# Input projection over four prompt tiles and one tile that holds the samples' high and low halves side by side

## The chip, the cores and the metric

The kernel runs on one core of one Trainium2 chip. The metric is the device time of one execution in microseconds (us), as the median of several runs. The matrix engine is TensorE (PE in the profile, PEld its loads of the stationary operand), the others are VectorE (DVE), ScalarE (ACT), GpSimd (POOL) and SyncE (SP), which here only issues DMA transfers.

## The reference, cut to what matters

The reference is one step of a decoder layer for 512 prompt tokens and 64 sample tokens (8 sequences of 8). Both groups go through the same weights:

```python
def mix_inputs(x, pos, g_attn, w_in, w_gate_up, b_gate):
    xn = rms_norm(x, g_attn)
    gq, gk, gv, gr, ga, sq, sk, sv = split_cols(xn @ w_in)     # 2048 x 4368 weights
    ...
    log_a = log_sigmoid(ga @ w_gate_up + b_gate) / GLA_TAU
    sq, sk = rope(sq, pos), rope(sk, pos)

def layer_sample(...):
    q, k, v, log_a, gr, sq, sk, sv = mix_inputs(...)
    o_gla, s_fin = gla_recurrent(q, k, v, log_a, s_gla)        # linear attention with a state
    o_swa, new_k, new_v = swa_sample(sq, sk, sv, c_k, c_v, attn_sinks)   # window attention with a cache
    ...
```

Then come an output projection, a second norm, and a layer of 16384 experts of which 128 per token are chosen. All is in float32. The change touches the product `xn @ w_in` and the place where the sample attention reads its rows.

## The kernel before, in words

The kernel runs stage after stage: norm and transpose, input projection (`project`), attention of the prompt, attention of the samples (`attend`, called twice), output projection, expert queries, routing, experts, final norm. Each stage ends with a barrier of all engines.

**High and low halves.** TensorE multiplies in a rounded float32 format. To keep float32 accuracy each operand is split into a high part (the value rounded by a ScalarE copy) and a low part (the rest, by a subtraction). A product is three passes: high x high, high x low, low x high (`PASSES`); low x low is left out. `product` (L104) runs over 16 chunks of 128 of the contraction and issues 48 matmuls that all add into one bank of PSUM.

**The projection** (L237 and below). The 4368 output columns are cut into 14 slices of 312. The 576 tokens, kept transposed in `c.act[HI]` and `c.act[LO]`, are the stationary operand: five tiles of 128 tokens, at a stride of 112 (`STRIDE`), so that neighbouring tiles overlap by 16 tokens (4 x 112 + 128 = 576). The weights' slice moves, 312 columns at a time. Per slice PE does 5 tiles x 48 matmuls. SP loads the raw weights of the next slice; ACT makes the high half of them (L284), DVE the low half (L297). DVE copies each finished bank to `out` (L306), and GpSimd stores it into the scratch array `proj` in DRAM (L271): 112 rows of tiles 0 to 3, 128 of tile 4, so that no row is stored twice. PE waits for `split` (the slice's halves) at the start of a slice and for `moved` (the bank is free) before a tile; its waits come in program order.

**The sample attention** (`attend(nc, c, "sample")`). SP loads the samples' 64 rows of `proj` into `cur` in four pieces (L684): columns GA0..V0 (gate input, q, k), SQ0..SV0 (window queries and keys) together with a small table for the rotation, V0..SQ0 (v and output gate), SV0..PROJ (window values). Each piece has a semaphore (`qk_here`, `s_here`, `vr_here`, `sv_here`). ACT issues ten small loads of constants in the meantime. DVE clears two tiles (L900, L901) and then waits for all constants; PE waits for them as well, transposes the gate input (L1098), and DVE copies it (L914): from there a chain of gate logarithms, sums, exponentials (ACT), a reciprocal of 64 x 1024 (L931) and products (L936 to L939) runs on DVE, until PE computes with the recurrent state (L1139, L1147). GpSimd rotates the window queries and keys (L764, six steps). The recurrent state, 4 MB, is loaded to `state` by SP (L712) after the constants and `vr_here`.

Of the kernel before, what the change touches and what calls it, by code (L numbers as in the profile page):

```python
# [5 lines left out]
ALU = mybir.AluOpType  # L6
# [3 lines left out]
F32R = mybir.dt.float32r  # L10
U32 = mybir.dt.uint32

P = 128
D = 2048
KC = D // P
SEQ = 512
DEC_BATCH, DEC_SEQ = 8, 8
SAMPLES = DEC_BATCH * DEC_SEQ
TOKENS = SEQ + SAMPLES
PROMPT_TILES = SEQ // P  # L20
TILES = 5
STRIDE = (TOKENS - P) // (TILES - 1)
W_IN_SLICES = 14
HALF = TOKENS // 2
HI, LO = 0, 1
# [8 lines left out]
SWA_HEADS, HD, KV = 16, 64, 2  # L34
# [5 lines left out]
GA0 = 0  # L40
Q0 = GA0 + GATE_RANK
K0 = Q0 + GLA_HEADS * DK
V0 = K0 + GLA_HEADS * DK
R0 = V0 + GLA_HEADS * DV
SQ0 = R0 + GLA_HEADS * DV
SK0 = SQ0 + SWA_HEADS * HD
SV0 = SK0 + KV * HD
PROJ = SV0 + KV * HD
# [46 lines left out]
def in_pairs(eng, count, step):  # L95

    with eng.Fori(0, count // 2 - 1) as i:
        for s in range(2):
            step(i * 2 + s, s, True)
    for s in range(2):  # L100
        step(count - 2 + s, s, s == 0)


def product(pe, out, stationary, moving):  # L104

    for k in range(KC):
        for n, (a, b) in enumerate(PASSES):
            last = pe.matmul(out, stationary(a, k), moving(b, k), start=(k == 0 and n == 0),  # L108
                             stop=(k == KC - 1 and n == len(PASSES) - 1))
    return last  # L110
# [123 lines left out]
            each_tile(pe, turn)  # L234


def project(nc, c, name, weights, first, dst):  # L237

    ctx, sb, sem = stage(nc)
    with ctx:
        slices, cols = weights.shape[0], weights.shape[3]
        raw = [first[0], sb(name + "_raw", [P, KC, cols])]
        w = [[first[1 + part], sb(name + tag, [P, KC, cols], F32R)] for part, tag in ((HI, "_hi"), (LO, "_lo"))]
        out = sb(name + "_out", [P, TILES, cols])
        raw_here = [sem(f"{name}_raw_here{s}") for s in range(2)]
        rounded, split = sem(name + "_rounded"), sem(name + "_split")
        stored, out_free = [[sem(f"{name}_{x}{t}") for t in range(TILES)] for x in ("stored", "out_free")]  # L250
        summed, moved = sem(name + "_summed"), sem(name + "_moved")
        block = ctx.enter_context(nc.Block())

        @block.sync
        def _(sp):
            def load(n, s, more):
                if more:
                    sp.wait_ge(split, n + 1)
                    sp.sem_inc(c.held, 1)
                    sp.dma_start(raw[1 - s][:, :, :], weights[bass.ds(n + 1, 1)].rearrange("a p k n -> (a p) k n")).then_inc(raw_here[1 - s], 16)  # L260

            in_pairs(sp, slices, load)

        @block.gpsimd
        def _(pool):
            def store(n, s, more):
                for t in range(TILES):
                    rows = P if t == TILES - 1 else STRIDE
                    pool.wait_ge(moved, n * TILES + (TILES + t + 1))
                    pool.sem_inc(c.held, 1)  # L270
                    pool.dma_start(dst[t * STRIDE:t * STRIDE + rows, bass.ds(n * cols, cols)], out[0:rows, t, :]).then_inc(stored[t], 16)  # L271
                for t in range(TILES):
                    pool.wait_ge(stored[t], n * 16 + 16)
                    pool.sem_inc(out_free[t], 1)

            in_pairs(pool, slices, store)

        @block.scalar
        def _(act):
            def hi(n, s, more):  # L280
                if more:
                    act.wait_ge(raw_here[1 - s], n * 8 + (16 - 8 * s))
                    act.wait_ge(summed, n * TILES + 2 * TILES)
                    act.activation(w[HI][1 - s][:, :, :], raw[1 - s][:, :, :], ACT.Copy).then_inc(rounded, 1)  # L284

            in_pairs(act, slices, hi)

        @block.vector
        def _(dve):
            dve.sem_inc(split, 2)  # L290
            dve.sem_inc(moved, TILES)
            for t in range(TILES):
                dve.sem_inc(out_free[t], 1)

            def lo(n, s):
                dve.wait_ge(rounded, n)
                dve.tensor_tensor(w[LO][s][:, :, :], raw[s][:, :, :], w[HI][s][:, :, :].bitcast(F32),  # L297
                                  ALU.subtract).then_inc(split, 1)

            def move(n, s, more):  # L300
                if more:
                    lo(n + 1, 1 - s)
                for t in range(TILES):
                    dve.wait_ge(out_free[t], n + 1)
                    dve.wait_ge(summed, n * TILES + (2 * TILES + t + 1))
                    dve.tensor_copy(out[:, t, :], c.bank[:, t, 0:cols]).then_inc(moved, 1)  # L306

            in_pairs(dve, slices, move)

        @block.tensor  # L310
        def _(pe):
            pe.sem_inc(summed, 2 * TILES)

            def products(n, s, more):
                pe.wait_ge(split, n + 2)
                for t in range(TILES):
                    pe.wait_ge(moved, n * TILES + (t + 1))
                    product(pe, c.bank[:, t, 0:cols], lambda part, k: c.act[part][:, k, t * STRIDE:t * STRIDE + P],
                            lambda part, k: w[part][s][:, k, :]).then_inc(summed, 1)

            in_pairs(pe, slices, products)

# [154 lines left out]
def attend(nc, c, kind):  # L477
# [15 lines left out]
    def sb(name, shape, dt=F32):  # L493
        return sb_(kind + "_" + name, shape, dt)

    def sem(name, n=1):

        s = sem_(kind + "_" + name)
        per[id(s)] = n
        return s  # L500

    with ctx:
# [46 lines left out]
        else:  # L549
# [6 lines left out]
            k2 = sb("k2", [P, 2, KV, 2, HD])  # L556
            k2_old = sb("k2_old", [DEC_SEQ, 2, KV, 2, HD])

        const_here = sem("const_here")


# [31 lines left out]

        block = ctx.enter_context(nc.Block())
        b0, b2, b3, b7 = (c.bank[:, n, :] for n in (0, 2, 3, 7))

        def wait(eng, s, i, n=None):

# [80 lines left out]
        def _(sp):  # L679
            def load(t, dst, src, here, first, end):  # L680

                at = bass.ds(t * P, P) if prompt else slice(SEQ, TOKENS)
                sp.sem_inc(c.held, 1)
                sp.dma_start(dst[0:T, first:end], src[at, first:end]).then_inc(here, 16)  # L684

            def load_swa(t):
                load(t, cur, c.d.proj, s_here, SQ0, SV0)
                load(t, trig, c.d.trig, s_here, 0, HD)

            load(0, cur, c.d.proj, qk_here, GA0, V0)  # L690
            load_swa(0)
            load(0, cur, c.d.proj, vr_here, V0, SQ0)
            load(0, cur, c.d.proj, sv_here, SV0, PROJ)
            if prompt:
                with sp.Fori(0, turns - 1) as i:
                    wait(sp, rope_step, i)
                    load_swa(i + 1)
                    wait(sp, gated, i)
                    wait(sp, er_ready, i)
                    load(i + 1, cur, c.d.proj, qk_here, GA0, V0)  # L700
                    wait(sp, o_ready, i)
                    wait(sp, silu_ready, i)
                    load(i + 1, cur, c.d.proj, vr_here, V0, SQ0)
                    wait(sp, kept, i)
                    load(i + 1, cur, c.d.proj, sv_here, SV0, PROJ)
                for s in (gla_heads_ready, swa_heads_ready, kept, state_ready):
                    wait(sp, s, turns - 1)
            else:
                sp.wait_ge(const_here, all_consts)
                sp.wait_ge(vr_here, 16)  # L710
                sp.sem_inc(c.held, 1)
                sp.dma_start(state[:], c.d.state_in.rearrange("b h d v -> d b h v")).then_inc(old_here, 16)  # L712
                for dst, src in ((k_old, ck), (v_old, cv)):
                    sp.dma_start(dst[:], src[:, 0:DEC_SEQ, :].rearrange("b t f -> t b f")).then_inc(old_here, 16)
                for dst, src in ((k_new, ck), (v_new, cv)):
                    sp.dma_start(dst[0:WINDOW - DEC_SEQ, :, :],
                                 src[:, DEC_SEQ:WINDOW, :].rearrange("b t f -> t b f")).then_inc(old_here, 16)
# [24 lines left out]
        def _(pool):  # L742
# [45 lines left out]
            def turn(i, more):  # L788
# [13 lines left out]
                pool.tensor_copy(mask[:, :], mask_all[:, :]).then_inc(kept, 1)  # L802
                end_turn(pool, i)

            rope(0)
            if prompt:
                with pool.Fori(0, turns - 1) as i:
# [91 lines left out]
        def _(dve):  # L899
            dve.memset(ga_t[:, :], 1.0).then_inc(first_ready, 1)  # L900
            dve.memset(q_spread[:, :, :], 0.0).then_inc(first_ready, 1)  # L901
            if prompt:
                dve.memset(state[:, 0, :, :], 0.0).then_inc(first_ready, 1)
                dve.memset(k_t[:, :, 0:WINDOW], 0.0).then_inc(first_ready, 1)
            dve.wait_ge(const_here, all_consts)
            dve.wait_ge(first_ready, 5 if prompt else 2)
            dve.sem_inc(c.held, 1)
# [1424 lines left out]
```

## Time and profile before

| what | value |
|---|---|
| median of 3 runs | 4011.97 us (4008.87 to 4014.4) |
| the profiled execution | 4016.56 us, its span 4014.9 us |
| PE busy | 3706.2 us, 92% of the span |
| DVE, ACT, POOL busy | 61%, 30%, 48% |
| projection's matmuls | from 53.8 to 537.4 us |
| prompt attention | from about 547 to 800 us |
| sample attention | from about 800 us to about 940 us |

A stage of this kernel begins when the last engine of the stage before has ended, so its time is that of the chain that ends last in it. In the profile "L108" is the line of the matmul in the helper `product`, "128*128" after it the rows and columns of the stationary operand, and "128x312" the moving one. "PEclk" is the clock granted to TensorE as a share of full speed (1.00 is 2.4 GHz, 0.50 is 1.2 GHz).

### The profile page before, as it was taken

The numbers are of one execution on the slowest core, as the hardware profiler recorded it, in microseconds if no ns is written. First come the engines' busy times: TensorE is split into PE (matmuls) and PEld (weight loads), VectorE is DVE, ScalarE is ACT, GpSimd is POOL, SyncE is SP. The second block draws the span as 40 slices with busy tenths as digits, with TensorE's granted clock in tenths as the row PEclk, the third lists the DMA queues.
The fourth block names the chain that finished last, engine by engine and source line by source line (L and its number), as shares of the span: only waits on it lengthen the run. The fifth ranks groups of instructions, "written<-read, shape, count | busy, mean of one in ns | idle before, by whom it ended". The sixth has DMA issues, their size and how long they took to land. (4 is left out here: it accounts for less than half of the span.)

```text
span 4014.9 us, 68430 instructions
## 1 busy us (share of the span) xinstructions
PE 3706.2 (92%) x26360; PEld 3625.3 (90%) x26360; DVE 2429.9 (61%) x3100; ACT 1222.9 (30%) x1291; POOL 1944.7 (48%) x1188
## 2 busy tenths in 40 slices
PE   6999966668969999999999999999999999999995
PEld 6999955547969999999999999999999999999995
DVE  5222235540031999444445887888887887888886
ACT  3111123311221445444443333333323333333322
POOL 1000032213432999988883545544554555555551
PEclk8999977768989999999999999999999999999998
DMA  4222111042312656555557888888888888888877
GB/s 163 98 98 96 47 50 42 22 119 106 131 67 80 210 193 212 194 215 205 198 204 262 304 314 308 313 305 304 320 305 295 315 325 308 313 307 303 321 283 246
DMA packets 255947, 853.25 MB, mean 213 GB/s; under 512 B 26816, under 2 KB 109440, under 8 KB 182626
## 3 DMA queue, kind: packets, MB, share of 16 engines
q1 hardware_dynamic: 183662, 544.96, 38.6%
q0 software_dynamic: 48704, 282.27, 18.1%
q10 hardware_dynamic: 23476, 24.61, 1.8%
q8 instruction: 67, 1.10, 0.1%
q14 instruction: 38, 0.31, 0.0%
HBM read 787.50 MB, written 64.20 MB: 212 GB/s over the span
## 5 line engine op out<-in xcount | busy, mean ns | idle before, releaser
L1882 POOL DMA_INDIRECT fetched<-in_v,at x256 | 526.9, 2058 | 636.7 <-DVE total L1999 583.1
L1999 DVE SCALAR_TENSOR_TENSOR total<-fetched,coef_s,total 128x2048 f32<-128x2048 f32 x256 | 600.8, 2347 | 76.8 <-issue 66.4
L2067 PE MATMUL bank<-coef_hi,act_hi 128*128 128x320 f32 x2048 | 633.9, 310 | 11.2 <-DVE y_t L2005 5.6
L2067 PE MATMUL bank<-coef_hi,act_lo 128*128 128x320 f32 x2048 | 632.5, 309 | 0.0
L2067 PE MATMUL bank<-coef_lo,act_hi 128*128 128x320 f32 x2048 | 632.4, 309 | 0.0
L1886 POOL DMA_INDIRECT hot_s<-hot_scratch,at x256 | 399.6, 1561 | 241.3 <-DVE coef_s L1992 164.2
L2067 PEld LDWEIGHTS bank<-coef_hi,act_hi 128*128 128x128 f32 x2048 | 384.7, 188 | 12.7 <-DVE act_lo L1975 6.1
L1934 ACT ACTIVATE hot<-bank 128x320 f32<-128x320 f32 x128 | 55.9, 437 | 1112.7 <-PE bank L108 1103.6
L1559 POOL TENSOR_SCALAR rt_first<-rt_number,picks_t 128x128 f32<-128x128 f32 x320 | 356.1, 1128 | 66.9 <-PE bank L1765 66.8
L108 PE MATMUL bank<-act_hi,first_hi 128*128 128x320 f32 (+1 forms) x1152 | 354.6, 308 | 34.7 <-DVEq L1332 30.3
L2067 PEld LDWEIGHTS bank<-coef_lo,act_hi 128*128 128x128 f32 x2048 | 384.6, 188 | 0.0
L2067 PEld LDWEIGHTS bank<-coef_hi,act_lo 128*128 128x128 f32 x2048 | 384.5, 188 | 0.0
L1975 DVE TENSOR_TENSOR act_lo<-raw_v,act_hi 128x2048 fp32r<-128x2048 f32 x128 | 293.5, 2293 | 132.5 <-ACT act_hi L1930 132.4
L108 PE MATMUL bank<-act_lo,first_hi 128*128 128x320 f32 (+1 forms) x1152 | 354.4, 308 | 0.0
L108 PE MATMUL bank<-act_hi,first_lo 128*128 128x320 f32 (+1 forms) x1152 | 354.0, 307 | 0.0
L108 PE MATMUL bank<-act_lo,other_hi 128*128 128x320 f32 (+1 forms) x1152 | 352.9, 306 | 0.0
L108 PE MATMUL bank<-act_hi,other_hi 128*128 128x320 f32 (+1 forms) x1152 | 352.8, 306 | 0.0
L108 PE MATMUL bank<-act_hi,other_lo 128*128 128x320 f32 (+1 forms) x1152 | 352.7, 306 | 0.0
L1750 PE MATMUL bank<-act_hi,first_hi 128*128 128x256 f32 x1024 | 289.8, 283 | 7.0 <-POOL first_lo L1550 3.9
L1750 PE MATMUL bank<-act_hi,other_hi 128*128 128x256 f32 x1024 | 287.3, 281 | 0.1
L1750 PE MATMUL bank<-act_hi,first_lo 128*128 128x256 f32 x1024 | 287.0, 280 | 0.0
L1750 PE MATMUL bank<-act_lo,first_hi 128*128 128x256 f32 x1024 | 286.9, 280 | 0.0
(390 smaller groups left out, 9694.8 us busy)
## 6 DMA issues: line engine op xcount, KB each, us to landing
raw_v<-in_v SPq DMA_DIRECT2D x128, 1024.0 KB, 6.7
first_raw<-in_u_t SPq DMA_DIRECT2D x107, 1024.0 KB, 5.0
other_raw<-in_u_t SPq DMA_DIRECT2D x106, 1024.0 KB, 5.2
rt_raw<-in_u_t SPq DMA_DIRECT2D x43, 1024.0 KB, 5.0
gates_scratch<-rt_space SPq DMA_DIRECT2D x5, 4096.0 KB, 12.2
gates<-gates_scratch SPq DMA_DIRECT2D x64, 320.0 KB, 7.2
proj_raw<-in_w_in SPq DMA_DIRECT2D x7, 2496.0 KB, 10.0
mh_raw<-in_w_out SPq DMA_DIRECT2D x16, 1024.0 KB, 4.8
```

Source lines behind the costliest of these rows:

```text
L108: last = pe.matmul(out, stationary(a, k), moving(b, k), start=(k == 0 and n == 0), stop=(k == KC - 1 and n == len(PASSES) - 1))
L1559: last = pool.tensor_scalar(first[:, n % 2, t, :], number[:, :], c.picks_t[:, 0, at:at + 1], c.picks_t[:, 2, at:at + 1], ALU.is_equal, ALU ...
L1750: last = pe.matmul(c.bank[:, 5 + s, 0:SPARSE], u[a][s][:, k, :], c.act[b][:, k, 0:SPARSE], start=(k == 0 and n == 0), stop=(k == KC - 1 an ...
L1882: pool.indirect_dma_start(fetched[:, k % 2, :], None, c.d.v, bass.IndirectOffsetOnAxis(ap=at[:, s, k:k + 1], axis=0)).then_inc(fetched_her ...
L1886: pool.indirect_dma_start(hot_s[:, k:k + 1], None, row_elements, bass.IndirectOffsetOnAxis(ap=at[:, s, FETCH + k:FETCH + k + 1], axis=0)). ...
L1934: act.activation(hot[:, r, :], c.bank[:, r % 2, 0:DENSE], ACT.Gelu).then_inc(hot_ready, 1)
L1975: dve.tensor_tensor(v_slot(LO, s), raw_v[:, s].rearrange("e r (a d) -> e (r a) d", d=SPARSE), v_slot(HI, s).bitcast(F32), ALU.subtract).th ...
L1999: dve.scalar_tensor_tensor(out=total[:, :], in0=fetched[:, k % 2, :], scalar=coef_s[:, k:k + 1], in1=total[:, :], op0=ALU.mult, op1=ALU.ad ...
L2067: last = pe.matmul(c.bank[:, 4 + m, 0:DENSE], v_chunk(a, q % 2, r, m), coef[z][:, r, :], start=(r == 0 and n == 0), stop=(r == ROWS - 1 an ...
```

## The change

- The tiles of the projection no longer overlap: tiles 0 to 3 are prompt tokens 0..511, in tiles of 128, with `product` as before.
- Tile 4 is for the 64 samples alone. Two GpSimd copies build `pair`, for each of the 16 chunks the samples' high half in columns 0..63 and their low half in columns 64..127. One matmul of `pair` against the weights' high half gives high x high in PSUM rows 0..63 and low x high in rows 64..127. A second matmul, of the 64 high columns against the weights' low half, adds high x low to rows 0..63. So there are 32 matmuls instead of 48 for this tile.
- The lower rows (low x high) aren't added there. They are stored in a second piece of scratch (`sample_low`, over the array `gates`), by one more DMA per slice.
- The sample attention loads both parts, the second into `low_part` (over the tile of the recurrent state), and adds them in four pieces: two on DVE, two on GpSimd. `qk_here`, `vr_here`, `s_here` and `sv_here` are now signalled by these additions, and the load of the state waits for all four.

```diff
+def sample_low(c):
+    return c.d.gates[0].rearrange("j i t -> (j i t)")[0:SAMPLES * PROJ].rearrange("(t n) -> t n", n=PROJ)
...
         @block.gpsimd
         def _(pool):
             def store(n, s, more):
                 for t in range(TILES):
-                    rows = P if t == TILES - 1 else STRIDE
+                    rows = SAMPLES if t == PROMPT_TILES else P
...
+                    if t == PROMPT_TILES:
+                        pool.dma_start(sample_low(c)[:, bass.ds(n * cols, cols)], out[SAMPLES:P, t, :]).then_inc(stored[t], 16)
...
+            for part in (HI, LO):
+                pool.tensor_copy(pair[:, :, part * SAMPLES:(part + 1) * SAMPLES], c.act[part][:, :, SEQ:TOKENS]).then_inc(paired, 1)
             in_pairs(pool, slices, store)
...
         @block.tensor
         def _(pe):
+            pe.wait_ge(paired, 2)
             pe.sem_inc(summed, 2 * TILES)
+
+            def sample_product(s):
+                both, upper = c.bank[:, PROMPT_TILES, 0:cols], c.bank[0:SAMPLES, PROMPT_TILES, 0:cols]
+                for k in range(KC):
+                    first, last = k == 0, k == KC - 1
+                    if last:
+                        pe.matmul(upper, c.act[HI][:, k, SEQ:TOKENS], w[LO][s][:, k, :], start=False, stop=False)
+                    done = pe.matmul(both, pair[:, k, :], w[HI][s][:, k, :], start=first, stop=last)
+                    if not last:
+                        pe.matmul(upper, c.act[HI][:, k, SEQ:TOKENS], w[LO][s][:, k, :], start=False, stop=False)
+                return done
...
-                    product(pe, c.bank[:, t, 0:cols], lambda part, k: c.act[part][:, k, t * STRIDE:t * STRIDE + P],
-                            lambda part, k: w[part][s][:, k, :]).then_inc(summed, 1)
+                    if t < PROMPT_TILES:
+                        last = product(pe, c.bank[:, t, 0:cols], lambda part, k: c.act[part][:, k, t * P:(t + 1) * P],
+                                       lambda part, k: w[part][s][:, k, :])
+                    else:
+                        last = sample_product(s)
+                    last.then_inc(summed, 1)
...
+        def add_parts(eng, first, end, here):
+            eng.wait_ge(parts_here[first], 32)
+            eng.tensor_tensor(cur[0:T, first:end], cur[0:T, first:end], low_part[:, first:end], ALU.add).then_inc(here, 16)
...
+            def load_parts(first, end):
+                sp.dma_start(cur[0:T, first:end], c.d.proj[SEQ:TOKENS, first:end]).then_inc(parts_here[first], 16)
+                sp.dma_start(low_part[:, first:end], sample_low(c)[:, first:end]).then_inc(parts_here[first], 16)
...
+            else:
+                load_parts(GA0, V0)
+                load_parts(SQ0, SV0)
+                load(0, trig, c.d.trig, s_here, 0, HD)
+                load_parts(V0, SQ0)
+                load_parts(SV0, PROJ)
...
                 sp.wait_ge(const_here, all_consts)
+                sp.wait_ge(qk_here, 16)
+                sp.wait_ge(s_here, 32)
                 sp.wait_ge(vr_here, 16)
+                sp.wait_ge(sv_here, 16)
...
+            if not prompt:
+                add_parts(pool, SQ0, SV0, s_here)
+                add_parts(pool, SV0, PROJ, sv_here)
             rope(0)
...
+            else:
+                add_parts(dve, GA0, V0, qk_here)
+                add_parts(dve, V0, SQ0, vr_here)
             dve.wait_ge(const_here, all_consts)
```

## Rows read from the trace of the kernel before

**Rows 1.** Stretches: us, busy (count) of PE PEld DVE ACT POOL; PEclk, DMA share, GB/s.
```profile
53.80:58.80 5.00, 4.98 (x19) 4.99 (x20) 0.00 (x0) 0.00 (x0) 0.00 (x0) 0.50 0.83 304
58.80:537.40 478.60, 478.57 (x3343) 478.31 (x3341) 101.72 (x82) 56.96 (x13) 37.39 (x69) 1.00 0.24 87
```

**Rows 2.** Timeline of PE around 839: start, us, engine, line, shapes.
```profile
838.70 0.59 PE L1139 MATMUL bank<-sample_state,sample_q_spread 128*64 128x256 f32 x2
...
838.91 0.38 PE L1139 MATMUL bank<-sample_state,sample_q_spread 128*64 128x256 f32 x1
839.22 0.43 PE L1137 MATMUL bank<-sample_cur,sample_inner 64*64 64x256 f32 x1
...
839.49 0.38 PE L1137 MATMUL bank<-sample_cur,sample_inner 64*64 64x256 f32 x1
```

**Rows 3.** Timeline of PE around 852, same columns.
```profile
851.73 0.48 PE L1147 MATMUL bank<-sample_cur,sample_spare 64*128 64x256 f32 x1
...
852.05 0.38 PE L1147 MATMUL bank<-sample_cur,sample_spare 64*128 64x256 f32 x1
```

**Rows 4.** Timeline of PE and its weight loads around 670 and 822.
```profile
669.84 0.27 PE L1159 MATMUL bank<-ident,prompt_o_norm 128*128 128x128 f32 x1
670.04 0.34 PE L1247 MATMUL bank<-prompt_probs_t,prompt_v_before 128*64 128x128 f32 x2
...
821.10 1.06 PE L1107 MATMUL bank<-sample_log_a,sample_suf 64*64 64x512 f32 x1
...
821.95 1.06 PE L1107 MATMUL bank<-sample_log_a,sample_suf 64*64 64x512 f32 x1
822.94 0.38 PE L1109 MATMUL bank<-sample_ind,sample_log_a 64*128 64x8 f32 x1
...
822.94 0.28 PEld L1109 LDWEIGHTS bank<-sample_ind,sample_log_a 64*128 64x128 f32 x1 [1.61 <-issue]
```

**Rows 5.** Timeline of PE around 902, transposes.
```profile
902.19 0.42 PE L1231 MATMUL bank<-ident,sample_scores 128*128 128x128 f32 x1
902.40 0.42 PE L1233 MATMUL bank<-ident,sample_scores 128*8 128x128 f32 x1
```

**Rows 6.** Timeline of PE around 906, pairs of short matmuls.
```profile
906.36 0.30 PE L1258 MATMUL bank<-sample_spare,sample_v_old 8*64 8x32 f32 x2
906.59 0.24 PE L1256 MATMUL bank<-sample_spare,sample_v_new 128*64 128x32 f32 x1
```

**Rows 7.** GpSimd's copies (groups by form: count, busy us, mean ns), its last store.
```profile
L801 POOL COPY prompt_k_t<-prompt_k_t 128x256 f32<-128x256 f32 x4 | 1.6, 403 | 0.0
...
L800 POOL COPY prompt_v_before<-prompt_cur 128x128 f32<-128x128 f32 x4 | 1.2, 291 | 56.0 <-PE bank L1248 56.0
...
538.56 0.56 POOL L271 DMA_DIRECT2D proj_scratch<-proj_out  x1 [6.36 <-DVE proj_out L306]
```

**Rows 8.** Sample attention: a load, landings, DVE, stretches (as rows 9); a long subtraction.
```profile
802.98 1.19 SPq L684 DMA_DIRECT2D sample_cur<-proj_scratch  x2
...
DMA to landing us min/median/max: 4.0/6.2/6.2
...
811.35 0.21 DVE L914 COPY sample_ga_t<-bank 16x64 f32<-16x64 f32 x1 [8.00 <-PE bank L1098]
...
801.40:809.90 8.50, 0.00 (x0) 0.50 0.80 167
812.00:825.00 13.00, 7.05 (x14) 0.50 1.07 334
...
L1975 DVE TENSOR_TENSOR act_lo<-raw_v,act_hi 128x2048 fp32r<-128x2048 f32 x128 | 293.5, 2293 | 132.5 <-ACT act_hi L1930 132.4
```

**Rows 9.** Three stretches: us, PE busy (matmuls), PEclk, DMA share, GB/s.
```profile
838.60:852.30 13.70, 13.70 (x61) 1.00 0.24 70
857.50:860.95 3.45, 2.81 (x14) 1.00 0.00 0
860.95:864.40 3.45, 3.45 (x10) 0.50 0.00 0
```

More of the change, by code:

```diff
@@ L251, in project @@
         summed, moved = sem(name + "_summed"), sem(name + "_moved")
+        pair = sb(name + "_pair", [P, KC, 2 * SAMPLES], F32R)
+        paired = sem(name + "_paired")
         block = ctx.enter_context(nc.Block())
@@ L267, in store @@
                 for t in range(TILES):
-                    rows = P if t == TILES - 1 else STRIDE
+                    rows = SAMPLES if t == PROMPT_TILES else P
                     pool.wait_ge(moved, n * TILES + (TILES + t + 1))
                     pool.sem_inc(c.held, 1)
-                    pool.dma_start(dst[t * STRIDE:t * STRIDE + rows, bass.ds(n * cols, cols)], out[0:rows, t, :]).then_inc(stored[t], 16)
+                    pool.dma_start(dst[t * P:t * P + rows, bass.ds(n * cols, cols)], out[0:rows, t, :]).then_inc(stored[t], 16)
+                    if t == PROMPT_TILES:
+                        pool.dma_start(sample_low(c)[:, bass.ds(n * cols, cols)], out[SAMPLES:P, t, :]).then_inc(stored[t], 16)
                 for t in range(TILES):
-                    pool.wait_ge(stored[t], n * 16 + 16)
+                    pool.wait_ge(stored[t], n * 32 + 32 if t == PROMPT_TILES else n * 16 + 16)
                     pool.sem_inc(out_free[t], 1)
+            for part in (HI, LO):
+                pool.tensor_copy(pair[:, :, part * SAMPLES:(part + 1) * SAMPLES], c.act[part][:, :, SEQ:TOKENS]).then_inc(paired, 1)
             in_pairs(pool, slices, store)
@@ L557, in attend @@
             k2_old = sb("k2_old", [DEC_SEQ, 2, KV, 2, HD])
+            low_part = state[:, :, :, :].rearrange("p n h v -> p (n h v)")[0:T, 0:PROJ]
+            parts_here = {first: sem(f"part_here{first}") for first in (GA0, V0, SQ0, SV0)}
         const_here = sem("const_here")
@@ L688, in load_swa @@
                 load(t, trig, c.d.trig, s_here, 0, HD)
[L690 to L693, printed above, removed]
+            def load_parts(first, end):
+                sp.dma_start(cur[0:T, first:end], c.d.proj[SEQ:TOKENS, first:end]).then_inc(parts_here[first], 16)
+                sp.dma_start(low_part[:, first:end], sample_low(c)[:, first:end]).then_inc(parts_here[first], 16)
+            if prompt:
+                load(0, cur, c.d.proj, qk_here, GA0, V0)
+                load_swa(0)
+                load(0, cur, c.d.proj, vr_here, V0, SQ0)
+                load(0, cur, c.d.proj, sv_here, SV0, PROJ)
+            else:
[4 more added lines that the diff above has]
+                load_parts(SV0, PROJ)
             if prompt:
```

## The prediction

> **What bounds the kernel now.** I read the stretches of the input projection first, since that is where the change takes work away. Two stretches cover it [rows 1]: in the second the matrix engine (PE) is busy for 478.57 of 478.60 us, at a granted clock of 1.00, in 3343 matmuls, so one is issued every 478.6 / 3343 = 0.1432 us. Nothing else is near: in the same stretch VectorE is busy 101.72 us and GpSimd 37.39 us. PE's number of matmuls is this stage's time. Then I read PE's own timeline where the shape of the stationary operand changes from one matmul to the next [rows 2 to 4], because the new sample tile does that all the time and the old projection never does: all its matmuls are 128*128 (rows*columns of the stationary operand). Last I read the start of the sample attention, where the parts are added.
>
> **The projection: what goes.** Before, 14 slices x 5 tiles x 48 matmuls = 3360. After, a slice has 4 x 48 for the prompt and 32 for the samples (16 with the high and low halves side by side, 16 with the high half alone against the weights' low half). So 14 x 16 = 224 go: 224 x 0.1432 = **-32.1 us**, if the remaining ones keep the spacing.
>
> **The projection: what comes in.** In the sample tile, stationary operands of 128 columns and of 64 columns take turns. The order is both, upper, both, upper, and at the last k upper, both: 15 changes from 128 to 64 columns and 15 from 64 to 128 per slice. What does a change cost?
> - At full clock, matmuls of 64 columns follow each other every 0.21 to 0.22 us (838.70, 838.91; I reckon with 0.216). Then the rows of the operand change from 128 to 64, and the next starts 0.31 us later (839.22) and the one behind it 0.27 us after that (839.49) [rows 2]. A change thus costs about 0.093 before the first matmul of the new shape and 0.051 behind it, 0.144 us. I read it as: the next weights are not loaded while the last matmul still runs, but only after it. The row of the load says so too: at 822.94 a load starts together with its matmul after 1.61 us in which none was loaded [rows 4].
> - Into a 128-column operand the second part is larger: 851.73 to 852.05 is 0.32 us, 0.104 above 0.216 [rows 3]. So 0.093 + 0.104 = 0.197 us.
> - These change rows, or rows and columns. Two places change columns alone. At full clock 128*128 to 128*64 takes 0.20 us (669.84 to 670.04) behind transposes that at this clock should be spaced at about half their 0.213 us of the lower one [rows 4, 5]: +0.09 again. At the lower clock 64*64 to 64*128 takes 0.99 us (821.95 to 822.94) where the same work without a change takes 0.85 (821.10 to 821.95): +0.135 [rows 4]. So I take the change of columns at the price of the others.
>
> Per slice 15 x 0.144 + 15 x 0.197 = 5.12 us; x 14 = **+71.6 us**. The bounds: nothing per change [rows 5] (the first rival below), and 0.23 us, the time that two matmuls of 32 columns take together where each pair changes shape (906.36 to 906.59) [rows 6]; x 420 = 97 us. I take 71.6, as it comes from the rows nearest in moving length. Of the stage, -32.1 + 71.6 = +39.5 us, and a sample tile takes 32 x 0.143 + 5.12 = 9.7 us instead of 6.9.
>
> The Trainium skill has this rule (TensorEngine Tiling (Array Packing), Key Properties): a change of the tiling mode, as opposed to the tile alone, drains the engine. By that rule the trace agrees for every change of shape shown in rows 2 to 4. It gives no price. The same page (Restrictions) says that column tiling can't be had together with the transpose mode on 4-byte inputs, which would explain why rows 5, both transposes, show no such cost; no run here separates that yet.
>
> **The start of the projection.** PE now waits for two GpSimd copies of 128 x 1024 elements. It had started at 53.8 [rows 1]. COPY takes 0.291 us for 128 elements and 0.403 for 256 [rows 7]: 0.87 ns an element above a fixed part, so 1.07 us each and **+2.2 us** in all with the signal. Bounds: 1.2 (the lost time is at the lower clock [rows 1], 0.26 us a matmul against 0.143) and 3.3 (8 x 0.403). Queued behind the copies on GpSimd is only the first store, some 8 us later; behind PE's wait are the summed signal, thus ACT's conversion of the next slice, which waits for its load until 10 us later anyway. SP's load of the next slice isn't behind it.
>
> **Stores.** One more store per slice. A store's issue takes GpSimd 0.56 us [rows 7]; 13 of them lie under PE's work on the next slice, and DVE waits for out_free only a slice later. The last lies behind the last matmul: **+0.55 us** (0 to 1).
>
> **The prompt attention** reads the same rows of the same scratch: 0.
>
> **The sample attention.** Before, SP issues four loads of the projection (1.12 MB); those with V and R and the last are issued from 802.98 and land up to 6.2 us later, 809.2, at 167 GB/s in that stretch [rows 8]. DVE copies the gate inputs that PE turns at 811.35, just after the last constant is there [rows 8]. Now the low parts double the bytes: 1.09 MB more up to V and R. At 167 GB/s that is 6.5 us, at the 334 GB/s of the state load 3.3 us [rows 8]. So V and R land at 812.5 to 815.7. DVE adds them (64 x 2048 elements; 2.29 us by the row of the same length [rows 8]) before it waits for the constants, and only then copies its gates: 814.8 to 818.0, i.e. 3.5 to 6.6 us later. I take **+5.0 us**. The bounds: 0.2, if the transfers went no slower (809.2 + 2.3), and 10, if the add also waits for GpSimd, which now adds and rotates in the same time. Everything behind it shifts with it: the reciprocal and then qg, kg, ke are one chain on DVE. Two other waits move and stay under it. The state load is issued after the adds, not at 811; PE's first use of it is at the end of that same chain, so both shift by as much. GpSimd adds SQ..SV0 and the last 128 columns ahead of the rotation, whose keys SP needs only behind its cache loads, which come later too.
>
> **Sum.** -32.1 + 71.6 + 2.2 + 0.55 + 5.0 = +47.3 us. The profiled execution took 4016.56 us (4014.9 of it the span, 1.7 around it), so 4063.8 of its kind; the median of the runs shown is 4.6 lower, 4011.97, and with it **4059 us**.
>
> **Rivals.**
> - *The change of columns is free* (the price fails altogether). For it: alternating 128*128 and 128*8 operands run at 0.213 us each, without any gap [rows 5], and weights are loaded ahead there. Against: these are transposes, and rows 4 show the cost for columns in matmuls. Then -32.1 + 7.8 = -24.3: 3988 us, faster. It decides at 24.3 / 420 = 0.058 us per change: below that the kernel is faster.
> - *Half a price*: the engine waits for the end of the last matmul, but the weights' load hides in it. 420 x 0.093 = 39.1; -32.1 + 39.1 + 7.8 = +14.8: 4027 us. For it: no row shows a stream where each single matmul changes columns. Against: in rows 2 and 3 both parts are there.
> - *The clock falls in the sample tile.* With 9.7 us for 32 matmuls PE streams under half of the time there. For it: behind a stretch with 14 matmuls of half-filled rows in 3.45 us the granted clock fell from 1.00 to 0.50 [rows 9]. Against: in the stretch before, shapes changed too and it held at 1.00 over 13.7 us [rows 9]. The price: in 5.0 us at the lower clock 19 matmuls are done, 0.26 us each [rows 1], so 2.3 us are lost in each 5; one such fall per slice, up to two: 14 x 2.3 to 4.6 = 32 to 64 us more: 4091 to 4123, say 4107 us. The Trainium skill (TensorE: Matmul & The Clock Gate, Part 1) says that the clock is gated by how busy PE has been recently; rows 9 agree with that in kind.
>
> **Chances.** My forecast 0.50, clock falls 0.20, half a price 0.15, free 0.15. The forecast's own range, with the bounds of its terms, is 4035 to 4080. The range for 8 in 10 leaves out the free case and the top of the clock case: 4018 to 4120. A difference of 0.2% (8 us) is about what can be told from none. Faster by more: the free case, 0.15. Within: the lowest part of half a price, 0.04. Slower: 0.81.
>
> **What would show it.** In the changed kernel: 448 matmuls of the sample tiles, 224 of them with 64 columns; the next start 0.34 us behind a "both" (0.143 + 0.104 + 0.093) and 0.29 us behind an "upper" (0.143 + 0.051 + 0.093), or 0.143 behind each if the free rival is right; PE's weight loads starting with their matmul and not ahead of it; a sample tile of about 9.7 us; the stage ending at some 580 (537.4 + 2.2 + 39.5) instead of 513 with free changes; the granted clock at 1.00 through each slice, or 0.50 in each sample tile. At the sample attention, DVE's copy of the gates 5 us later against the stage's first load. I am wrong if the 128 to 64 change leaves the spacing as it is, or if ACT or DVE turn up as what PE waits for between slices.

## The result, and the profile of the changed kernel

The changed kernel takes **3998.26 us** (median of 6 runs, 3994.82 to 4004.03), the kernel before beside it 4013.02 (6 runs, 4008.87 to 4019.1): a ratio of 0.9962, interval 0.9952 to 0.9973. It is faster, by 10.8 to 19.3 us. The forecast was 4059 in a range of 4018 to 4120: wrong in sign, and outside the range.

PE alone between two weight shapes in a sample tile (after, the timeline of PE and of its weight loads; start, us, engine, line, shapes):

```profile
86.98 0.31 PE L333 MATMUL bank<-slice_hi,proj_pair 128*128 128x312 f32 x1
87.12 0.30 PE L335 MATMUL bank<-slice_lo,act_hi 128*64 128x312 f32 x1
87.27 0.31 PE L333 MATMUL bank<-slice_hi,proj_pair 128*128 128x312 f32 x1
...
86.98 0.13 PEld L335 LDWEIGHTS bank<-slice_lo,act_hi 128*64 128x64 f32 x1
87.13 0.19 PEld L333 LDWEIGHTS bank<-slice_hi,proj_pair 128*128 128x128 f32 x1
87.27 0.14 PEld L335 LDWEIGHTS bank<-slice_lo,act_hi 128*64 128x64 f32 x1
```

The matmuls start 0.14 to 0.15 us apart, at 128 columns and at 64, which is the spacing of the old projection [rows 1]. The weights of the next matmul are loaded when the one before it starts (the load for the matmul of 87.12 starts at 86.98), so PE never waits for them. Over the whole stage, the matmuls behind the 420 changes start 0.1429 us after the one before (mean of the trace at full clock). A change of columns costs nothing here, where the forecast had put 0.144 and 0.197 us.

The same in stretches (after; us, busy and count of each engine, granted clock, DMA share, GB/s). The first answers to the two of [rows 1] together, then the part at the lower clock and the rest:

```profile
56.10:508.70 452.60, 452.58 (x3136) 450.54 (x3136) 101.68 (x82) 56.90 (x13) 44.63 (x82) 0.99 0.26 97
...
56.11:61.50 5.39, 5.39 (x21) 5.39 (x22) 0.00 (x0) 0.00 (x0) 0.00 (x0) 0.50 0.98 419
61.50:508.70 447.20, 447.19 (x3117) 445.14 (x3116) 101.68 (x82) 56.90 (x13) 44.63 (x82) 1.00 0.26 93
...
86.00:90.70 4.70, 4.70 (x35) 4.57 (x34) 0.48 (x1) 0.00 (x0) 0.54 (x1) 1.00 0.10 34
```

There are 3136 matmuls instead of 3360, PE never pauses, 447.20 / 3117 = 0.1435 us each, and the clock holds at 1.00 through the sample tiles, so the rival with a falling clock did not happen either. From PE's first projection matmul to its last, the stage went from 483.55 us (53.82 to 537.37) to 452.58 (56.11 to 508.69), -31.0.

Where the rest of it went, read from the first and last matmul of each stage in the two timelines. The profiled span fell by 18.8 us (4014.9 to 3996.1):

| Term | forecast, us | measured, us |
|---|---|---|
| PE's start of the projection (53.82, 56.11) | +2.2 | +2.3 |
| 224 matmuls fewer | -32.1 | -31.0 |
| 420 changes of columns | +71.6 | in the line above |
| last projection matmul to the prompt attention's first (21.49, 23.38) | +0.55 | +1.9 |
| prompt attention (233.93, 233.16) | 0 | -0.8 |
| prompt's last matmul to the samples' last (134.44, 143.12) | +5.0 | +8.7 |
| sample attention's end to the head merge (15.29, 15.95) | 0 | +0.7 |
| sum at the head merge (942.52, 924.30) | +47.3 | -18.2 |

Only the third line decides the sign. Of the 31.0, 1.1 less than the 32.1 forecast, the shortfall lies in the prompt tiles: in the two traces their matmuls are 0.1432 us apart before and 0.1436 after, which is 1.1 us over 2680 of them. The kernels below that keep the sample tile's 32 matmuls as they are have 0.1436 too, the others 0.1431 to 0.1433; why is open. The line of the prompt attention can't be told from none: its code is unchanged, and in the traces of this document it takes between 233.2 and 236.1 us.

PE's start and the stores of the last slice (before, then after; timeline of GpSimd and PE):

```profile
53.82 0.62 PE L108 MATMUL bank<-slice_hi,act_hi 128*128 128x312 f32 x1 [7.43 <-DVEq L291]
...
53.60 1.04 POOL L286 CAST proj_pair<-act_hi 128x1024 fp32r<-128x1024 f32 x1 [6.17 <-POOLq L73]
54.59 1.03 POOL L286 CAST proj_pair<-act_lo 128x1024 fp32r<-128x1024 f32 x1
...
56.11 0.62 PE L108 MATMUL bank<-slice_hi,act_hi 128*128 128x312 f32 x1 [9.43 <-POOL proj_pair L286]
...
509.87 0.55 POOL L278 DMA_DIRECT2D proj_scratch<-proj_out  x1 [4.03 <-DVE proj_out L317]
510.41 0.55 POOL L280 DMA_DIRECT2D gates_scratch<-proj_out  x1
```

After, the second copy is what PE waited for last. 1.04 and 1.03 us are the 1.07 of the forecast. The bracket is PE's idle time since the last matmul of the norm stage, 7.43 us before and 9.43 after: the wait for the pair is worth 2.0 of the 2.3 us. The other 0.3 is in the norm stage, whose last matmul ends at 46.39 in the one profile and at 46.68 in the other.

The sample attention (before, timeline of SP's queue and DVE, then after, with GpSimd's last step of the rotation; these answer to [rows 8]):

```profile
800.82 1.42 SPq L684 DMA_DIRECT2D sample_cur<-proj_scratch  x2
...
818.60 0.68 DVE L924 TENSOR_TENSOR sample_log_a<-sample_low,sample_mag 64x512 f32<-64x512 f32 x1 [3.58 <-ACT sample_mag L828]
819.21 0.68 DVE L929 TENSOR_SCALAR sample_er<-sample_er 64x1024 f32<-64x1024 f32 x1
```
```profile
773.20 0.58 SPq L728 DMA_DIRECT2D sample_cur<-proj_scratch  x1
...
788.98 2.28 DVE L631 TENSOR_TENSOR sample_cur<-sample_cur,sample_state 64x2048 f32<-64x2048 f32 x1 [9.21 <-DMA sample_state<-gates_scratch]
791.19 0.20 DVE L971 COPY sample_ga_t<-bank 16x64 f32<-16x64 f32 x1
793.45 0.68 DVE L973 TENSOR_SCALAR sample_low<-bank 64x512 f32<-64x512 f32 x1 [2.06 <-PE bank L1158]
798.43 1.28 DVE L981 TENSOR_TENSOR sample_log_a<-sample_low,sample_mag 64x512 f32<-64x512 f32 x1 [3.58 <-ACT sample_mag L882]
799.65 1.88 DVE L986 TENSOR_SCALAR sample_er<-sample_er 64x1024 f32<-64x1024 f32 x1
...
799.35 1.63 POOL L815 TENSOR_TENSOR sample_roped<-sample_rt 64x576 f32<-64x576 f32 x1 [0.18 <-POOL sample_rt L815]
```

From the stage's first load to DVE's copy of the gates it is 17.99 us, before 10.53 (800.82 to 811.35): the addition of V and R waits 9.21 us for the low parts, takes 2.28 and only then lets the gates through. Behind that DVE's two operations at 798.43 and 799.65 took 1.28 and 1.88 us, where before both took 0.68.

### The profile page after: what moved, and what is told of

Its sections match the earlier page's. It is cut to its first block and busy times, and to the rows that moved or that the text cites. A ratio compares the mean times of both kernels' runs of the same rounds, so it can differ in the third digit from the quotient of the medians.

```text
span 3996.1 us, 68032 instructions
## 1 busy us (share of the span) xinstructions
PE 3679.9 (92%) x26136; PEld 3597.9 (90%) x26136; DVE 2435.8 (61%) x3102; ACT 1222.5 (31%) x1291; POOL 1938.9 (49%) x1206
## 5 line engine op out<-in xcount | busy, mean ns | idle before, releaser
L1943 POOL DMA_INDIRECT hot_s<-hot_scratch,at x256 | 381.2, 1489 | 241.2 <-DVE coef_s L2049 164.3
```

Of the source, the lines that this page charges most:

```text
L1943: pool.indirect_dma_start(hot_s[:, k:k + 1], None, row_elements, bass.IndirectOffsetOnAxis(ap=at[:, s, FETCH + k:FETCH + k + 1], axis=0)). ...
```

## The experiments

The forecast had read its price from matmuls that all work on full float32 operands, where the projection's are rounded to fp32r. In these profiles a full float32 matmul stands as two records, a rounded one as one. Two theories were to be told apart: *A*, the price belongs to full float32; *B*, it belongs to a change of the operand's rows, not of its columns. The two runs of shapes and the last one ran once each.

**Shapes with rounded operands.** The sample tile's 32 matmuls get other shapes, by turns (in even slices 128*128 with 64*128, then 64*128 with 64*64; in odd ones 128*64 with 64*64, then 128*128 with 64*64), with one full one at the end of the even slices and at the start of the odd ones; it leaves out part of the projection's sums.

```diff
-                    done = pe.matmul(both, pair[:, k, :], w[HI][s][:, k, :], start=first, stop=last)
...
+                for n, (rows, width) in enumerate(order):
+                    k = n // 2 % KC
+                    a, b = pair[0:rows, k, 0:width], w[HI][s][0:rows, k, :]
...
+                    done = pe.matmul(c.bank[0:width, PROMPT_TILES, 0:cols], a, b, start=n == 0, stop=n == len(order) - 1)
```

> The changed kernel, but the sample tile's 32 or 33 matmuls take other shapes, all on the rounded operands, so that the samples' projection is not computed. Even slices: 128*128 and 64*128 in turn (8 pairs), then 64*128 and 64*64 in turn (8 pairs). Odd slices: 128*64 and 64*64 in turn, then 128*128 and 64*64 in turn. Theory A (a change of shape costs only with operands in full float32, which is all that the trace of before showed it for; rounded operands pay nothing): 0.143 us from each start to the next in all four patterns, a tile of 4.6 to 4.8 us. Theory B (a change of the number of rows costs, in either format, a change of columns alone does not): 0.29 to 0.34 us at each change of rows, 0.143 in the pattern 64*128 / 64*64; the even tile some 7 us, the odd one 9 us, and the projection some 14 x 3.4 = 47 us longer than in the changed kernel.

4107.15 us. Its weight loads (timeline; the bracket is the idle time before a load):

```profile
88.57 0.19 PEld L335 LDWEIGHTS bank<-slice_hi,proj_pair 128*128 128x128 f32 x1 [0.15 <-issue]
88.91 0.18 PEld L335 LDWEIGHTS bank<-slice_hi,proj_pair 64*128 64x128 f32 x1 [0.15 <-issue]
89.25 0.19 PEld L335 LDWEIGHTS bank<-slice_hi,proj_pair 128*128 128x128 f32 x1 [0.15 <-issue]
...
286.40 0.13 PEld L335 LDWEIGHTS bank<-proj_hi,proj_pair 128*64 128x64 f32 x1 [0.16 <-issue]
286.69 0.13 PEld L335 LDWEIGHTS bank<-proj_hi,proj_pair 64*64 64x64 f32 x1 [0.15 <-issue]
```

Medians of start to start at full clock, over all slices: 338 and 337 ns between 128*128 and 64*128, 285 and 282 between 128*64 and 64*64, 337 and 283 between 128*128 and 64*64; but 141 and 146 between 64*128 and 64*64 (only 6 and 4 pairs, as most of that pattern ran at the lower clock) and 141 from 128*128 to 128*64 (7 pairs). A change of rows costs 0.14 to 0.20 us with rounded operands too, a change of columns alone nothing. *A* falls as the only reason; the price of the forecast, 0.144 and 0.197, is met for rows to within a few ns. The clock also fell, in the sample tile of every slice. The projection took 559.7 us instead of 452.6, where *B* had asked for some 47 more; the rest goes with the lower clock. The first fall (stretches):

```profile
82.00:92.00 10.00, 10.00 (x51) 7.67 (x50) 0.48 (x1) 0.00 (x0) 0.54 (x1) 1.00 0.14 51
92.00:99.00 7.00, 7.00 (x29) 6.33 (x27) 0.48 (x1) 2.42 (x1) 1.09 (x2) 0.51 0.03 6
```

**Shapes with full float32 operands.** The same edit with `a, b = a.bitcast(F32), b.bitcast(F32)`, and lists of shapes with changes of columns among them; it leaves out part of the sums too.

> The same with the operands read as full float32, where each matmul stands in the profile as two records (312 columns: 0.26 us each, by 0.216 for 256). Even slices: 128*128 and 128*64 in turn (8 pairs), then 64*128 and 64*64 in turn. Odd slices: eight 128*128, then 128*128 and 64*128 in turn (6 pairs), then 128*64 and 64*64 in turn (5 pairs). The samples' projection is not computed. Theory A: at each change, rows or columns, the starts lie 0.09 further apart before and 0.05 (into 64 columns) or 0.10 (into 128 columns) behind, 0.14 to 0.20 us per change, also for 128*128 / 128*64; none in the uniform eight. Theory B: no extra time in 128*128 / 128*64 nor in 64*128 / 64*64, only where the rows change.

4256.13 us. Without a change the records follow at 263 ns each. Weight loads where columns alone change:

```profile
299.58 0.19 PEld L335 LDWEIGHTS bank<-slice_hi,proj_pair 128*64 128x64 f32 x2 [0.42 <-issue]
300.25 0.30 PEld L335 LDWEIGHTS bank<-slice_hi,proj_pair 128*128 128x128 f32 x2 [0.48 <-issue]
```

One matmul of each shape takes 0.67 to 0.72 us instead of 0.53. In medians, the matmul of the new shape starts 356 ns behind the last one (+93) for 128*128 to 128*64 and for 128*64 to 128*128, 353 for 64*128 to 64*64, and 352 to 356 where rows change; its second record follows after 313 ns in a 128*64 operand (+50) and 367 in a 128*128 one (+104). So in full float32 columns cost as much as rows, in the very parts that the forecast took from [rows 2, 3]: 0.093, 0.051 and 0.104. *B* falls there. Together the two runs say: rows cost in both formats, columns only in full float32, and [rows 2 to 4], all full float32, could not show the difference. What it is about the format stays open: the transposes of [rows 5] also work on full float32, but are one record each, and they pay nothing for a change of columns (0.213 us at the lower clock, with or without a change).

The clock did not follow the changes of rows here. In all seven odd slices, where rows change by turns, it held at 1.00 through 20.7 us of sample tile. It fell in three of the even ones, and each time in the second half, where all operands have 64 rows.

The Trainium skill has one rule for both (TensorEngine Tiling (Array Packing), Key Properties): a change of the tiling mode drains the engine. Whether each shape of operand is a mode of its own, it doesn't say. Read so, as the forecast did, rows agree with it in both formats, columns in full float32; for columns with rounded operands the measurement says otherwise, and it decides.

**48 matmuls of 64 columns.** Back to before (and the edit is against before), except that the prompt tiles no longer overlap and the sample tile has 64 columns instead of 128: no halves side by side, no second store, the sample attention as before.

```diff
+            def sample_product(s):
...
+                return product(pe, c.bank[0:SAMPLES, PROMPT_TILES, 0:cols], lambda part, k: c.act[part][:, k, SEQ:TOKENS],
+                               lambda part, k: w[part][s][:, k, :])
```

> One part of the change alone: tiles of 128 prompt tokens and a sample tile of 64 columns, but with all three passes (48 matmuls, 128*64), no pair, no second scratch; the sample attention as in the kernel before. If a matmul of 64 stationary columns takes as long as one of 128 (0.143 us), nothing is gained without the side by side: 4013 us, within 0.1% of before, the projection 483.5 us. If fewer columns made it shorter (0.130 us = 312 columns at full clock), 672 x 0.013 = 9 us less, 4004 us.

4014.91 us against 4014.34 (10 and 15 runs), ratio 1.000, 0.9991 to 1.0009. The timeline of PE in a sample tile:

```profile
88.03 0.30 PE L108 MATMUL bank<-slice_hi,act_lo 128*64 128x312 f32 x1
88.17 0.30 PE L108 MATMUL bank<-slice_hi,act_hi 128*64 128x312 f32 x1
88.31 0.30 PE L108 MATMUL bank<-slice_lo,act_hi 128*64 128x312 f32 x1
```

A matmul takes the same with half its columns empty (0.142 against 0.143 us). The whole gain is in the number of matmuls, none in leaving out the overlap.

**Later wait for the pair.** PE's wait for the two copies moves from the stage's start to the first sample tile, four tiles later.

```diff
-            pe.wait_ge(paired, 2)
             pe.sem_inc(summed, 2 * TILES)
...
                     else:
+                        pe.wait_ge(paired, 2)
                         last = sample_product(s)
```

> The changed kernel, PE's wait for the pair moved from the start of the projection to just before the first sample tile, where the copies have long ended. If the wait is what lets PE start at 56.1 instead of 53.8, it starts at 53.8 again and all behind is 2.3 us earlier by the profile (1.2 if only the work at the lower clock is won): about 3996.5 us, ratio to before 0.9955 to 0.996. If the copies only took the place of another late arrival, nothing changes: 3998.5 us.

3996.90 us (3994.64 to 3998.59, 4 runs), ratio 0.9954, 0.9937 to 0.997. PE's first matmul (timeline):

```profile
54.70 0.62 PE L108 MATMUL bank<-slice_hi,act_hi 128*128 128x312 f32 x1 [7.42 <-DVEq L302]
```

PE's idle time ahead of it is 7.42 us, as before (7.43), against 9.43: by the profile the move gives back the whole 2.0 us of the wait. That the start isn't back at 53.82 lies ahead of it: in this profile the norm stage's last matmul ended at 47.28, in before's at 46.39. By the times it is 1.4 us, less than the intervals can tell.

**Transfers without additions, additions without transfers.** The 7.5 us at the sample attention are two costs in a row, transfers and an addition. One kernel loads all low parts and adds 16 elements of each; the other loads 16 elements of each (so every load is still issued) and makes the whole additions (with the high part added to itself). Their outputs miss the low parts.

```diff
-            eng.tensor_tensor(cur[0:T, first:end], cur[0:T, first:end], low_part[:, first:end], ALU.add).then_inc(here, 16)
+            eng.tensor_tensor(cur[0:T, first:first + 16], cur[0:T, first:first + 16], low_part[:, first:first + 16], ALU.add).then_inc(here, 16)
```
```diff
-                sp.dma_start(low_part[:, first:end], sample_low(c)[:, first:end]).then_inc(parts_here[first], 16)
+                sp.dma_start(low_part[:, first:first + 16], sample_low(c)[:, first:first + 16]).then_inc(parts_here[first], 16)
```

> The changed kernel, the low parts loaded as before, but each addition in the sample attention covers only the first 16 columns, so most of the low x high part is left out. Theory 'the transfers': DVE's copy of the gate inputs comes about 15.5 us behind the stage's first load instead of 17.9 (only the 2.3 us addition goes), and 10.5 in the kernel before; so the doubled loads are worth 5 of the 7.4 us. Theory 'the additions': it comes back to 11 us.

> The changed kernel, the additions at full width, but with the first part itself as second operand, and of the low parts only 16 columns each are loaded; the low x high part is left out. Theory 'the transfers': DVE's copy of the gate inputs comes about 12 to 13 us behind the stage's first load (10.5 and up to 2.3 for the addition). Theory 'the additions': 17 us. In both DVE's steps up to qg keep the 1.7 us by which GpSimd's shifted rotation lengthens them if that clash needs only the additions ahead of the rotation, and lose them if the rotation starts early enough again.

3996.15 and 3996.58 us, one run each. From each trace the first load of the stage and the copy of the gates, transfers alone first:

```profile
776.56 0.58 SPq L728 DMA_DIRECT2D sample_cur<-proj_scratch  x1
...
792.47 0.21 DVE L971 COPY sample_ga_t<-bank 16x64 f32<-16x64 f32 x1 [0.35 <-PE bank L1155]
```
```profile
775.21 0.58 SPq L728 DMA_DIRECT2D sample_cur<-proj_scratch  x1
...
788.13 0.20 DVE L971 COPY sample_ga_t<-bank 16x64 f32<-16x64 f32 x1
```

15.91 and 12.92 us, where before has 10.53 and after 17.99. Of the +7.5 the transfers are 5.4 and what is left, 2.1, is the addition; the additions alone give 2.4. The path from the gates' copy to the operation behind the reciprocal, 15.16 us before, is 16.84 in after and 16.73 and 16.78 in these two, but 15.16 in the joined kernel below. So this +1.7 comes with the later GpSimd rotation, which meets DVE's two operations (row at 799.35 above), and it stays when either part is made small.

**The low rows added in the projection (joined).** This takes away what the table of the changed kernel shows as losses. The sample tile comes second in the slice (ORDER = 0, 4, 1, 2, 3), its low rows are moved down by a transfer on the chip and added by GpSimd under PE's next tiles, one store goes out, and the sample attention is as before. PE waits for the pair only ahead of its first sample tile. The edit is against before.

```diff
+                    if t == PROMPT_TILES:
+                        pool.sem_inc(c.held, 1)
+                        pool.dma_start(low[:, :], out[SAMPLES:P, t, :]).then_inc(lowered, 16)
+                        pool.wait_ge(lowered, n * 16 + 16)
+                        pool.tensor_tensor(out[0:SAMPLES, t, :], out[0:SAMPLES, t, :], low[:, :], ALU.add).then_inc(joined, 1)
+                        pool.wait_ge(joined, n + 1)
```

> The 32 matmuls kept, the rest of the cost taken away: the sample tile is second in each slice, GpSimd moves its lower rows to rows 0..63 by a transfer within the chip, adds them there and stores one result, all behind PE's other tiles; PE waits for the pair only before that tile; the sample attention is that of the kernel before. If the changed kernel's gain of 31 us in the projection was eaten by 2.3 us of pair, about 1.9 at the end of the stage and 8.7 in the sample attention, this one gives 4013 - 31 = 3982 us (ratio 0.992), some 16 us below the changed kernel. If the sample attention's loss came from something else that also moved (clock phases, the placement of the barrier), it stays: 3990 us or more.

**3983.11 us** (3980.68 to 3987.16, 5 runs), ratio 0.9921, 0.9908 to 0.9935: by its interval 26 to 37 us below before, and below the changed kernel too. GpSimd and DVE (timeline), and the stretch of the projection with its part at the lower clock:

```profile
77.03 0.54 POOL L276 DMA_DIRECT2D table<-proj_out  x1
85.70 0.84 POOL L278 TENSOR_TENSOR proj_out<-proj_out,table 64x312 f32<-64x312 f32 x1 [8.14 <-DMA table<-proj_out]
...
783.74 0.21 DVE L943 COPY sample_ga_t<-bank 16x64 f32<-16x64 f32 x1 [8.39 <-PE bank L1127]
...
55.23:58.10 2.87, 2.87 (x11) 2.87 (x12) 0.00 (x0) 0.00 (x0) 1.51 (x2) 0.50 0.74 230
...
55.00:507.00 452.00, 451.50 (x3136) 449.53 (x3136) 101.78 (x83) 56.91 (x13) 58.88 (x99) 1.00 0.26 98
```

GpSimd waits 8.14 us for the transfer that it issued at 77.03. PE doesn't wait for it: the stage takes 451.50 us, the changed kernel's 452.58. The gates are copied 10.93 us behind the first load (before 10.53).

**More shapes with rounded operands.** Which changes are free, and is a matmul with few rows slow by itself? Even slices: 128*128 with 128*32 by turns, then 128*64 alone; odd slices: 64*128 alone, then 64*128 with 32*128. Part of the sums is left out again.

```diff
+                for n, (row, rows, at, width) in enumerate(order):
+                    k = n // 2 % KC
+                    a, b = pair[row:row + rows, k, at:at + width], w[HI][s][row:row + rows, k, :]
```

> The changed kernel with other shapes in the sample tile, on rounded operands (the samples' projection is not computed). Even slices: 128*128 and 128*32 in turn, then sixteen 128*64 in a row. Odd slices: twelve 64*128 in a row, then 64*128 and 32*128 in turn. Theory B' (with rounded operands only a change of rows costs, at each change, and no shape is slow by itself): 0.143 us from start to start in both patterns of the even slices and within the twelve 64*128; 0.34 us at each step between 64*128 and 32*128; the granted clock falls in the odd slices, as it did where rows changed, and holds in the even ones. Rival (64 rows are slow by themselves, or only 128 against 64 rows costs): over 0.2 us within the twelve, or 0.143 between 64 and 32 rows.

4042.85 us beside 4019.21 of before, one run each. Medians at full clock: 143 and 144 ns between 128*128 and 128*32, 142 for 128*64 alone, 144 for 64*128 alone, 337 and 340 between 64*128 and 32*128. So 32 columns are as free as 64, 64 rows cost nothing by themselves, and the change of rows costs at every pair tried. The clock held through the seven even tiles, which change columns, and fell in the seven odd ones, which first have twelve matmuls of 64 rows and then change rows (stretches of an even and an odd slice, and what follows):

```profile
86.00:91.00 5.00, 5.00 (x38) 4.63 (x37) 0.72 (x2) 0.24 (x1) 0.54 (x1) 1.00 0.09 32
118.00:122.30 4.30, 4.30 (x22) 3.00 (x20) 0.48 (x1) 0.00 (x0) 0.54 (x1) 1.00 0.11 37
122.30:132.50 10.20, 10.20 (x29) 7.77 (x30) 0.78 (x2) 4.37 (x1) 1.08 (x2) 0.50 0.08 16
```

## Why the prediction was wrong

- **"So I take the change of columns at the price of the others."** This is the step that failed: +71.6 us measured as 0, and it alone turned -24.3 into +47.3. The forecast had seen that [rows 2, 3] change rows, or rows and columns, and bridged the gap with two places of [rows 4]. Both were full float32, where columns do cost (+93 ns in the shapes run). The only rows against it were the transposes of [rows 5]. That these were set aside as a special case, on a restriction that the Trainium skill names for transposes (TensorEngine Tiling (Array Packing), Restrictions), was the mistake of judgement: no transpose is needed for the free change, as the changed kernel shows.
- **The number of matmuls** was right: 224 x 0.1432 = 32.1 against 31.0. The remaining matmuls keep their spacing but for 0.0004 us in the prompt tiles, which is the 1.1.
- **The free rival** had the mechanism and named the point of decision, 0.058 us; it gave 3988. Of the 10.6 us between that and 3998.26, 6.1 are in the table (+1.1 in the projection's length, +0.1 and +1.4 around it, -0.8, +3.7, +0.7). Another 4.0 are that the medians differ by 14.8 and the profiled spans by 18.8, both inside the interval of 10.8 to 19.3, and 1.1 that before had a median of 4013.02 beside it, not 4011.97; -0.6 comes behind the head merge.
- **The start**: +2.2 against 2.0 for the wait itself (idle time 9.43 against 7.43, and 7.42 and 7.43 in the two kernels with the later wait), and 1.07 us a copy against 1.04 and 1.03. The 2.3 of the table has 0.3 of the norm stage in it.
- **The stores**: 0.55 each as forecast, but the prompt attention's first matmul comes 1.9 later, not 0.55. The joined kernel, with one store, has +1.0 there. What the rest is made of stays open.
- **The sample attention**: the order of waits was right (parts, addition, gates), the size too low: +7.5 at the copy of the gates against 5.0, above the 3.5 to 6.6 that the two rates gave, though inside the outer bound of 10. The addition took the 2.28 foreseen; the transfers were slow. From the first load to the last one landed, 773.20 to 788.98, it is 15.8 us against 8.4, 7.4 more where 3.3 to 6.5 had been put, and the stretch moved 168 GB/s, the slower of the two rates. And DVE's chain behind it takes 1.7 more, which the forecast had nowhere: its bound of 10 was for an addition that waits for GpSimd. Of these 9.2 us 8.7 are left at the stage's end.
- **Clock and half a price**: neither occurred. What the forecast feared of the clock can happen: with rounded operands it fell in all 14 sample tiles of the first run of shapes. That rows change isn't enough for it, as the odd slices of the full float32 run show, and so did [rows 9].

The joined kernel checks this account from the other side: with the early wait and the sample attention's costs taken out it has -32.05 in the projection's length, +1.4 at its start, +1.0 at its end and +0.2 in the sample attention, 27.8 earlier at the head merge (942.52 to 914.68), with +1.6 in the prompt attention. The +1.4 is all of the norm stage, whose last matmul ends at 47.80 there; PE's idle time behind it is 7.43, as before.

## What to carry to other kernels

A price read from one kind of matmul holds for that kind: before carrying it over, compare operand type, rows and columns of the row with those of the new code, and where one differs, give the case without the price a good share of the chance. With rounded operands, stationary operands of 128, 64 and 32 columns could alternate here for nothing (moving 312 columns) as long as their rows stayed the same; what counted was the number of matmuls. If halves have to be added later, add them in the stage that has idle engines, not at the head of a stage that waits for them.

## What the runs showed of the hardware that was not expected

- Changes of columns (128, 64, 32) are free in matmuls with fp32r operands (141 to 146 ns against 142 to 144 without one) and cost 93 ns ahead of the matmul and 50 or 104 behind its first record with full float32 ones; changes of rows cost 0.14 to 0.20 us in both.
- The time at the lower clock at a stage's start differs between executions, with the same matmuls issued: the clock rose 5.4 us behind PE's first matmul in after, 5.0 in before [rows 1], 3.9 with the later wait and 2.9 in joined. At 0.26 us a matmul against 0.143, 2.5 us less at the lower clock are 1.1 us, the difference in length between the projections of joined (451.50) and after (452.58).
- In both rounded runs with changes of rows, the granted clock fell to 0.50 while PE showed no pause in its records (4.30 busy of 4.30 us). In the full float32 run it held at 1.00 through all seven tiles that change rows by turns, and fell in three whose second half works on 64 rows alone. What of a fall is due to rows left empty and what to the waits between shapes was not separated.
- DVE operations took 1.28 and 1.88 us instead of 0.68 where GpSimd worked at the same time, but not each one: that at 793.45, which reads a PSUM bank, took 0.68 beside a GpSimd instruction of 793.10 to 794.48. The rows fit an operation that stands still until GpSimd's instruction is over. GpSimd's last two steps of the rotation end at 799.18 and 800.98, DVE's two operations 0.53 and 0.55 us later; with the later wait, with the transfers alone and with the additions alone it is 0.54 or 0.55 as well. GpSimd's addition of 64x128 elements took 2.02 us beside DVE's of 2.28, and 0.3 us behind DVE's end it was over. No run tests this.
